# A matrix-vector product on four column tiles: two column blocks side by side, turned by one product of eight columns

## The chip, the cores and the metric

The kernel runs on one core of a Trainium2 chip. The metric is the device time of one execution in microseconds. Engines: TensorE (PE for products, PEld for its weight loads), VectorE (DVE), ScalarE (ACT), GpSimd (POOL) and SyncE (SP), which only issues DMAs here. Each engine runs its own list of instructions in order, and they meet at semaphores.

## What is computed

Two transformer-like blocks run one behind the other over 256 tokens of width 1024, with a context of 256 tokens. Block one: a state-space branch, a pooling branch and a mixture of experts. Block two: two layers of feed-forward, gated linear attention with latent attention, and neighbourhood attention. The change touches only the conditioning: both blocks scale and shift their activations by vectors that come from two condition vectors `c` and `c_ctx`:

```python
mod_l = jnp.split((jax.nn.silu(c) @ w_ada[i] + b_ada[i])[:, None, :], 6, axis=-1)
mod_c = jnp.split((jax.nn.silu(c_ctx) @ w_ada[i] + b_ada[i])[None, None, :], 6, axis=-1)
...
mod_l = jax.nn.silu(c) @ ada_w[l] + ada_b[l]
mod_c = jax.nn.silu(c_ctx) @ ada_w[l] + ada_b[l]
```

`w_ada` is 1024 x 6144, `ada_w` is two matrices of 1024 x 9216, all fp32. The results are needed with the feature on the partition, as `mod1` and `mod2` (128 partitions x tiles x 2).

## The kernel before

The conditioning is cut into 96 chunks of 256 output columns, so two tiles of 128 outputs: 8 in job `first`, 16 in `later`, 36 in each of the two jobs of `ada2`. Job `first` is done before anything else (`T.finish(K.first)`), for the first activations wait for its result. The others are background work: each engine takes one step of the job list at fixed places of its own program (`T.step()`, `S.step()`, `V.step()`): behind each weight tile of a linear product, once per round of the state-space loop (`ssd_pe`, line 1082; 10 rounds in each of 4 groups), once per state and twice per level of the gated linear attention (`gla_pe`, lines 2608 and 2637).

One chunk takes these steps. SP loads its 1024 x 256 weights (1 MB) into one of the three `RAW` buffers of the ring (line 344), as soon as PE has read the tile three places earlier. PE multiplies: for each of the 8 blocks of 128 inputs, `CS[:, k, :]` (128 x 32; columns 0 to 3 are silu of `c`, `c_ctx` and those of block two, the other 28 are zero) is the stationary operand and the weights are the moving one. The output of block k goes to the 32 partitions from `32 * (k % 4)`, that is to one of four column tiles of the array; the products on the four tiles can run side by side. After it each quarter of the bank holds the sum over two blocks, in its rows 0 to 3, for 256 columns. ACT copies the bank to `mrow` (line 520). One step later PE turns it: for each half of the columns `mrow` is the stationary operand and `quarters` the moving one, a 128 x 4 matrix of ones and zeros that adds the four quarters; so 4 columns come out per tile, with the feature on the partition. DVE adds the bias into `mod` (line 530).

So within one step (`conditioning_pe`, line 485) PE does the turn of chunk s-1 and then the row of chunk s. The turn waits for ACT's copy, the row for the weights (`T.ring.landed(j)`) and for a free bank. Banks are handed out in turn, 6 or 8 of them. Every product goes through `T.mm` (line 188 in the profile), every ACT operation through line 313, DVE's `stt` is line 253. An fp32 product stands in the trace as two load records and two product records.

Of the kernel before, what the change touches and what calls it, by code (L numbers as in the profile page):

```python
# [6 lines left out]
F32 = mybir.dt.float32  # L7
# [3 lines left out]
ACT = mybir.ActivationFunctionType  # L11
AX = mybir.AxisListType
MUL, ADD, SUB, MIN, MAX = ALU.mult, ALU.add, ALU.subtract, ALU.min, ALU.max
# [164 lines left out]
class Tensor(Engine):  # L178
# [58 lines left out]
    def conditioning(self, job, s):  # L237
        conditioning_pe(self, self.K, job, s)
# [69 lines left out]
class Scalar(Engine):  # L308
# [3 lines left out]
    def act(self, o, a, f, **k):  # L312
        return self.e.activation(o, a, f, **k) if self.e else NOTHING  # L313
# [21 lines left out]
    def conditioning(self, job, s):  # L335
        conditioning_act(self, self.K, job, s)
# [148 lines left out]
def conditioning_pe(T, K, job, s):  # L485


    pe, act = K.pe, K.act
    if s:
        c = job.base + s - 1  # L490
        b, held = T.bank("turned", c)
        for h in held:
            T.wait_ge(*h)
        T.wait_ge(*act.of("row", c))
        for q in range(2):
            r = T.mm(b[:, 4 * q:4 * q + 4], K.mrow[c % 2][:, q * 128:q * 128 + 128], K.quarters[:, :], True, True)
        r.then_inc(*pe("turned", c))
    if s < job.n:
        c = job.base + s
        j, w = T.weights(job.name, job.lead, 0, 8, job.order[s] * 128, 256, False)  # L500
        T.wait_ge(*T.ring.landed(j))
        b, held = T.bank("row", c)
        for h in held:
            T.wait_ge(*h)
        for k in range(8):
            q = 32 * (k % 4)
            r = T.mm(b[q:q + 32, 0:256], K.CS[:, k, :], w[:, k, :], k < 4, k >= 4)
        r.then_inc(*pe("row", c))
        pe.note("w", T.ring.name, j)


def conditioning_act(S, K, job, s):
    pe, act = K.pe, K.act
    if s < job.n:
        c = job.base + s
        S.take()
        S.wait_ge(*pe.of("row", c))
        if c > 1:
            S.wait_ge(*pe.of("turned", c - 2))
        S.act(K.mrow[c % 2][:, :], K.ps("row", c)[:, 0:256], ACT.Copy).then_inc(*act("row", c))  # L520
        K.free(act, "row", c)


# [146 lines left out]
class Kern:  # L670
    def __init__(self, nc, dram, out, ctx):
# [7 lines left out]
        sb = self.sb  # L679
# [20 lines left out]
        self.mod1 = sb("mod1", [128, 48, 2], F32)  # L700
        self.mod2 = [sb(f"mod2{i}", [128, 72, 2], F32) for i in range(2)]
        self.CS = sb("CS", [128, 8, 32], F32)
        self.quarters = sb("quarters", [128, 4], F32)
        self.mrow = [sb(f"mrow{i}", [128, 256], F32) for i in range(2)]
        self.banks = [ctx.enter_context(nc.psum_tensor(f"ps{i}", [128, 512], F32)) for i in range(8)]
        half = (2, 8)
        self.first = Job("w_ada", None, (0, 8, 2, 10, 4, 12, 6, 14), 0, self.v("b_ada", 0, 48), self.mod1, (), 0)
# [22 lines left out]
    def sb(self, name, shape, dt, ctx=None):  # L730
        return (ctx or self.ctx).enter_context(self.nc.sbuf_tensor(name, shape, dt))
# [45 lines left out]
def setup_dve(V, K):  # L777

    dve, q = K.dve, K.quarters[:, :]
    V.fill(K.CS[:, :, :], 0.0).then_inc(*dve("cs zero"))  # L780
    V.wait_ge(K.loaded["first"], 32)
    V.tt(q, K.ident[:, 0:4], K.ident[:, 32:36], ADD).then_inc(*dve())
    for i in (64, 96):
        V.wait_ge(*dve.last)
        V.tt(q, q, K.ident[:, i:i + 4], ADD).then_inc(*dve("quarters"))
    for key, n in (("b_ada", 1), ("ada_b", 2)):
        for i in range(n):
            for g in ((1, 4), (1, 4, 7))[n - 1]:
                b = K.v(key, 72 * i + 8 * g, 8)
                V.ts(b, b, 1.0, None, ADD).then_inc(*dve())  # L790
            for g in ((), (2, 8))[n - 1]:
                b = K.v(key, 72 * i + 8 * g, 8)
                V.ts(b, b, 0.5, None, MUL).then_inc(*dve())
    V.wait_ge(*dve.last)
# [2721 lines left out]
```

## Time and profile before

| | |
|---|---|
| time, median of 3 runs | 3405.75 us (3403.57 to 3408.22) |
| time of the profiled execution | 3411.45 us |
| its span, first to last instruction | 3409.6 us |
| mean granted TensorE clock | 0.949 of full |
| PE busy | 3090.1 us (91%) |
| PE weight loads busy | 2345.2 us (69%) |
| DVE busy | 1422.5 us (42%) |
| ACT busy | 1091.6 us (32%) |
| POOL busy | 307.5 us (9%) |

Busy shares are over the whole span; the stages differ. By time: 0 to 50 us the chunks of `first`; 50 to 225 the linear products and convolutions of the state-space branch; 225 to 420 the state-space loop; to 1700 the rest of block one and the experts, and the first feed-forward part of block two; 1774 to 1900 the gated linear attention; then the rest. The profiled span lacks 1.85 us of that execution's own time, which lies around it. A duration in a row is that of the record; where several records of one kind overlap, a row of the timeline gives the time from the first start to the last end.

### The profile page before, as it was taken

How to read it: one execution, taken by the hardware profiler on the slowest of the kernel's cores; microseconds unless marked ns; L12 is line 12 of the kernel's file. 1: busy time of each engine (PE TensorE's matmuls, PEld its weight loads, DVE VectorE, ACT ScalarE, POOL GpSimd, SP SyncE). 2: the span in 40 equal slices, each digit the busy share in tenths (PEclk: the TensorE clock that was granted, in tenths of full speed). 3: DMA queues.
4: the chain of work that ended last, by engine and by line, in shares of the span. 5: the costliest groups of instructions: out<-in, count | busy, mean ns of one | idle time of the engine just before them, and what ended most of it. 6: DMA issues, size and time to landing. Idle time of an engine off the chain costs nothing.

```text
span 3409.6 us, 40973 instructions
## 1 busy us (share of the span) xinstructions
PE 3090.1 (91%) x17468; PEld 2345.2 (69%) x17468; DVE 1422.5 (42%) x2099; ACT 1091.6 (32%) x1579; POOL 307.5 (9%) x309
## 2 busy tenths in 40 slices
PE   6988899769999979999898798999989999897998
PEld 4765599745555547787676546878768787773898
DVE  4654554522222234333476454333243333436554
ACT  4443354322222223222342232322242222434433
POOL 0023470100000001000104000000010000300000
PEclk9987899869999989999999899999999999999999
DMA  7456754479999942232239321223222322310453
GB/s 221 156 187 198 225 167 133 121 280 385 395 395 392 387 184 85 77 112 67 82 122 294 97 74 50 96 83 106 74 87 87 99 85 88 136 62 0 131 179 99
DMA packets 415209, 537.16 MB, mean 158 GB/s; under 512 B 14340, under 2 KB 389924, under 8 KB 390308
## 3 DMA queue, kind: packets, MB, share of 16 engines
q1 hardware_dynamic: 415012, 534.38, 46.0%
q8 instruction: 142, 2.33, 0.3%
q14 instruction: 55, 0.45, 0.0%
HBM read 533.30 MB, written 1.05 MB: 157 GB/s over the span
## 4 chain that ended last, share of the span: by engine, by line
PE 82%; DVE 8%; ACT 4%; DMA 3%; issue 2%; SPq 0%; POOL 0%; DVEq 0%; ACTq 0%; POOLq 0%
PE ps L188 80%; PE ps L187 2%; DVE ar L243 2%; ACT ar L313 2%; DMA RAW<-in_ada_w 1%; DVE LR L243 1%; DVE ar L259 1%; ACT HR L313 1%; DMA RAW<-in_w_in 1%; PE ps L194 1%; DVE ar L262 0%; DVE ar L253 0%; DVE ar L249 0%; ACT arf1i L313 0%; ACT AH L313 0%
## 5 line engine op out<-in xcount | busy, mean ns | idle before, releaser
L188 PE MATMUL ps<-AH,HR 128*128 128x512 f32 (+1 forms) x2552 | 901.1, 353 | 64.7 <-DVE AL L243 39.9
L188 PE MATMUL ps<-AL,HR 128*128 128x512 f32 (+1 forms) x2552 | 887.2, 348 | 0.0
L188 PE MATMUL ps<-AH,LR 128*128 128x512 f32 (+1 forms) x2552 | 886.4, 347 | 0.0
L243 DVE TENSOR_TENSOR LR<-RAW,HR 128x2048 fp32r<-128x2048 f32 (+3 forms) x232 | 486.2, 2097 | 601.9 <-ACT HR L313 596.2
L313 ACT ACTIVATE HR<-RAW 128x2048 fp32r<-128x2048 f32 (+3 forms) x232 | 404.1, 1744 | 772.6 <-PE ps L188 666.3
L188 PEld LDWEIGHTS ps<-AH,HR 128*128 128x128 f32 x2552 | 491.3, 193 | 139.8 <-ACT arf1i L313 19.8
L188 PEld LDWEIGHTS ps<-AL,HR 128*128 128x128 f32 x2552 | 491.7, 193 | 59.9 <-issue 1.9
L188 PEld LDWEIGHTS ps<-AH,LR 128*128 128x128 f32 x2552 | 490.9, 192 | 59.0
L188 PE MATMUL ps<-ar 64*128 64x128 f32 (+9 forms) x1318 | 237.7, 370 | 61.7 <-ACT ar L313 26.8
L249 POOL TENSOR_SCALAR X<-X 128x512 f32<-128x512 f32 (+2 forms) x50 | 83.8, 1702 | 2266.0 <-ACT AH L313 1631.8
L188 PEld LDWEIGHTS ps<-ar 64*128 64x128 f32 (+2 forms) x1318 | 140.0, 188 | 147.9 <-issue 47.7
L253 DVE SCALAR_TENSOR_TENSOR X<-ps,mod,X 128x256 f32<-128x256 f32 x152 | 67.4, 480 | 324.5 <-PE ps L188 312.5
L243 POOL TENSOR_TENSOR ar<-ar 128x384 f32<-128x384 f32 (+5 forms) x138 | 151.0, 1103 | 297.8 <-DVE ar L243 117.1
L313 ACT ACTIVATE ar<-ar 128x384 f32<-128x384 f32 (+7 forms) x208 | 109.4, 557 | 164.7 <-DVE ar L249 53.7
L188 PE MATMUL ps<-BHf1i,HR 128*128 128x512 f32 x352 | 147.9, 420 | 11.6 <-DVE BLf1i L243 11.6
L313 ACT ACTIVATE ar<-ps 128x256 f32<-128x256 f32 (+4 forms) x190 | 89.2, 475 | 203.7 <-PE ps L188 195.6
L188 PE MATMUL ps<-BLf1i,HR 128*128 128x512 f32 x352 | 142.5, 405 | 0.0
L188 PE MATMUL ps<-BHf1i,LR 128*128 128x512 f32 x352 | 142.1, 404 | 0.0
L313 ACT ACTIVATE ar_few<-ps 128x512 f32<-128x512 f32 x64 | 47.0, 734 | 286.6 <-PE ps L188 286.6
L188 PE MATMUL ps<-RAW,CS 128*32 128x256 f32 x1536 | 127.4, 459 | 10.4 <-DMA RAW<-in_w_ada 8.2
L188 PE MATMUL ps<-BHf2i,HR 128*128 128x512 f32 (+1 forms) x352 | 124.4, 353 | 9.6 <-DVE BLf2i L243 9.6
L188 PE MATMUL ps<-BLf2i,HR 128*128 128x512 f32 (+1 forms) x352 | 120.4, 342 | 0.0
(181 smaller groups left out, 3778.9 us busy)
## 6 DMA issues: line engine op xcount, KB each, us to landing
RAW<-in_ada_w SPq DMA_DIRECT2D x72, 1024.0 KB, 5.8
RAW<-in_f1i SPq DMA_DIRECT2D x44, 1024.0 KB, 5.1
RAW<-in_f2i SPq DMA_DIRECT2D x44, 1024.0 KB, 5.1
RAW<-in_w_in SPq DMA_DIRECT2D x32, 1024.0 KB, 5.5
RAW<-in_w_ada SPq DMA_DIRECT2D x24, 1024.0 KB, 7.9
RAW<-in_w_eu SPq DMA_DIRECT2D x17, 1024.0 KB, 10.2
HF<-in_w_ed SPq DMA_DIRECT2D x17, 1024.0 KB, 9.2
LF<-in_w_eu SPq DMA_DIRECT2D x17, 1024.0 KB, 10.1
```

The lines of the kernel that those rows point to most:

```text
L187: return self.e.matmul(o, w, x, start=start, stop=stop, skip_group_check=True)
L188: return self.e.matmul(o, w, x, start=start, stop=stop)
L194: return self.e.transpose(o, a, self.K.ident[sp:sp + q, sp:sp + q])
L243: return self.e.tensor_tensor(o, a, b, op) if self.e else NOTHING
L249: return self.e.tensor_scalar(o, a, s1, None, o1)
L253: return self.e.scalar_tensor_tensor(out=o, in0=a, scalar=s, in1=b, op0=o1, op1=o2) if self.e else NOTHING
L259: return self.e.reciprocal(x, x) if self.e else NOTHING
L313: return self.e.activation(o, a, f, **k) if self.e else NOTHING
```

## The change

The row product is laid out anew. The four column tiles now take 128 columns each: tiles 0 and 1 the first 128 output columns of the chunk, tiles 2 and 3 the second 128. Of each pair one tile sums the input blocks 0 to 3 (tile 0, tile 2) and the other the blocks 4 to 7 (tile 1, tile 3). So there are 16 products of 128 columns where there were 8 of 256, and the bank is filled over 128 columns. ACT copies 128 columns, `mrow` is 128 x 128, and one product by `quarters`, now 128 x 8, adds the two half sums of each tile and turns both: columns 0 to 3 are those of the first tile, 4 to 7 those of the second. `quarters` is made by two additions that don't wait for each other, instead of three in a chain. DVE's reading of the turned bank is as it was.

```diff
--- before.py
+++ after.py
@@ -492,9 +492,7 @@
         for h in held:
             T.wait_ge(*h)
         T.wait_ge(*act.of("row", c))
-        for q in range(2):
-            r = T.mm(b[:, 4 * q:4 * q + 4], K.mrow[c % 2][:, q * 128:q * 128 + 128], K.quarters[:, :], True, True)
-        r.then_inc(*pe("turned", c))
+        T.mm(b[:, 0:8], K.mrow[c % 2][:, :], K.quarters[:, :], True, True).then_inc(*pe("turned", c))
     if s < job.n:
         c = job.base + s
         j, w = T.weights(job.name, job.lead, 0, 8, job.order[s] * 128, 256, False)
@@ -502,9 +500,11 @@
         b, held = T.bank("row", c)
         for h in held:
             T.wait_ge(*h)
-        for k in range(8):
-            q = 32 * (k % 4)
-            r = T.mm(b[q:q + 32, 0:256], K.CS[:, k, :], w[:, k, :], k < 4, k >= 4)
+        for k in range(4):
+            for q in range(4):
+                f = k + 4 * (q % 2)
+                r = T.mm(b[32 * q:32 * q + 32, 0:128], K.CS[:, f, :], w[:, f, q // 2 * 128:q // 2 * 128 + 128], k == 0,
+                         k == 3)
         r.then_inc(*pe("row", c))
         pe.note("w", T.ring.name, j)
 
@@ -517,7 +517,7 @@
         S.wait_ge(*pe.of("row", c))
         if c > 1:
             S.wait_ge(*pe.of("turned", c - 2))
-        S.act(K.mrow[c % 2][:, :], K.ps("row", c)[:, 0:256], ACT.Copy).then_inc(*act("row", c))
+        S.act(K.mrow[c % 2][:, :], K.ps("row", c)[:, 0:128], ACT.Copy).then_inc(*act("row", c))
         K.free(act, "row", c)
 
 
@@ -700,8 +700,8 @@
         self.mod1 = sb("mod1", [128, 48, 2], F32)
         self.mod2 = [sb(f"mod2{i}", [128, 72, 2], F32) for i in range(2)]
         self.CS = sb("CS", [128, 8, 32], F32)
-        self.quarters = sb("quarters", [128, 4], F32)
-        self.mrow = [sb(f"mrow{i}", [128, 256], F32) for i in range(2)]
+        self.quarters = sb("quarters", [128, 8], F32)
+        self.mrow = [sb(f"mrow{i}", [128, 128], F32) for i in range(2)]
         self.banks = [ctx.enter_context(nc.psum_tensor(f"ps{i}", [128, 512], F32)) for i in range(8)]
         half = (2, 8)
         self.first = Job("w_ada", None, (0, 8, 2, 10, 4, 12, 6, 14), 0, self.v("b_ada", 0, 48), self.mod1, (), 0)
@@ -779,10 +779,9 @@
     dve, q = K.dve, K.quarters[:, :]
     V.fill(K.CS[:, :, :], 0.0).then_inc(*dve("cs zero"))
     V.wait_ge(K.loaded["first"], 32)
-    V.tt(q, K.ident[:, 0:4], K.ident[:, 32:36], ADD).then_inc(*dve())
-    for i in (64, 96):
-        V.wait_ge(*dve.last)
-        V.tt(q, q, K.ident[:, i:i + 4], ADD).then_inc(*dve("quarters"))
+    for i in range(2):
+        V.tt(q[:, 4 * i:4 * i + 4], K.ident[:, 64 * i:64 * i + 4], K.ident[:, 64 * i + 32:64 * i + 36],
+             ADD).then_inc(*dve("quarters"))
     for key, n in (("b_ada", 1), ("ada_b", 2)):
         for i in range(n):
             for g in ((1, 4), (1, 4, 7))[n - 1]:
```

## Rows read from the trace of the kernel before

**Rows 1.** page, part 4: share of the ending chain by engine.
```profile
PE 82%; DVE 8%; ACT 4%; DMA 3%; issue 2%; SPq 0%; POOL 0%; DVEq 0%; ACTq 0%; POOLq 0%
```

**Rows 2.** groups by shape: names, shape, count | busy us, mean ns | idle.
```profile
L188 PE MATMUL ps<-RAW,CS 128*32 128x256 f32 x1536 | 127.4, 459 | 10.4 <-DMA RAW<-in_w_ada 8.2 <-DMA RAW<-in_ada_w 2.0
...
L188 PE MATMUL ps<-quarters,mrow 128*128 128x4 f32 x384 | 66.4, 279 | 41.6 <-ACT mrow L313 40.4 <-DVE ar L268 1.2
...
L188 PE MATMUL ps<-ar_few 128*128 128x64 f32 x512 | 60.6, 271 | 1.2 <-DVE ar_few L256 1.2
...
L313 ACT ACTIVATE mrow<-ps 128x256 f32<-128x256 f32 x96 | 36.6, 381 | 126.9 <-PE ps L188 109.2 <-DMA X<-in_ctxT 16.0
...
L313 ACT ACTIVATE ar<-ps 128x128 f32<-128x128 f32 x16 | 4.3, 270 | 6.4 <-PE ps L188 6.4
```

**Rows 3.** windows, `mrow` alone: stretch, length, PE, PEld, ACT busy, clock.
```profile
50.00:225.00 175.00, 6.55 (x48) 7.39 (x48) 4.79 (x13) 0.94 0.50 159
225.00:420.00 195.00, 28.82 (x160) 25.33 (x160) 14.99 (x39) 0.82 0.65 210
...
1800.00:1900.00 100.00, 17.88 (x112) 15.81 (x112) 10.74 (x28) 0.89 0.92 288
```

**Rows 4.** timeline, state-space round: start us, duration us, engine, operation, count.
```profile
243.67 0.61 PE L188 MATMUL ps<-quarters,mrow 128*128 128x4 f32 x4
...
244.21 0.59 PEld L188 LDWEIGHTS ps<-RAW,CS 128*32 128x32 f32 x16
244.21 1.07 PE L188 MATMUL ps<-RAW,CS 128*32 128x256 f32 x16
244.23 1.43 POOL L243 TENSOR_TENSOR X<-X,ar 128x256 f32<-128x256 f32 x2 [0.71 <-ACT X L313]
...
245.21 0.65 PE L188 MATMUL ps<-X,ar 128*64 128x256 f32 x4
...
245.61 1.32 POOL L243 TENSOR_TENSOR ar<-ar 128x384 f32<-128x384 f32 x1
...
247.07 0.27 PE L188 MATMUL ps<-quarters,mrow 128*128 128x4 f32 x1
```

**Rows 5.** chain of waits, state-space stage: start us, duration us, what.
```profile
227.22 35.05 PE ps L188 x312
```

**Rows 6.** timeline, linear stage.
```profile
115.60 0.50 PE L188 MATMUL ps<-quarters,mrow 128*128 128x4 f32 x4
...
117.04 0.50 PE L188 MATMUL ps<-AH,HR 128*128 128x512 f32 x1
```

**Rows 7.** chain of waits, first stage.
```profile
23.61 0.39 ACT mrow L313
...
27.00 0.38 ACT mrow L313
...
30.67 0.28 ACT mrow L313
```

**Rows 8.** chain of waits, stage from 1800.
```profile
1815.33 5.15 PE ps L188 x72
...
1821.02 5.15 PE ps L188 x72
...
1845.28 4.64 PE ps L188 x68
...
1849.93 7.33 DMA RAW<-in_ada_w
```

**Rows 9.** timeline, a turn at half clock in the state-space stage.
```profile
230.99 1.02 PE L188 MATMUL ps<-quarters,mrow 128*128 128x4 f32 x4
```

**Rows 10.** records of `ar`: duration min/median/max ns, first and last start.
```profile
L188 PE MATMUL ps<-ar x8: 272/272/324, 1783.5 to 1783.9; 128*64 128x128 f32 x8
```

**Rows 11.** timeline, the same records.
```profile
1783.49 0.66 PE L188 MATMUL ps<-ar 128*64 128x128 f32 x8 [0.23 <-DVE ar L256]
```

**Rows 12.** PE sequencer waits, 242.3 to 242.6: duration ns, first, last start.
```profile
L147 PEldq EVENT_SEMAPHORE  x2: 51/51/51, 242.4 to 242.5; - x2
```

## The prediction, made before the changed kernel was run

> **What bounds the kernel now.** I read the page first. TensorE (PE) makes up 82% of the chain that ended last, so a change to PE work counts wherever PE is what ends last [rows 1]. Then the groups of instructions by shape, for what the change touches: 1536 records of the row products, 384 of the turning products, 96 copies of `mrow` [rows 2]. That is 96 chunks; each fp32 product appears as two records (two passes), so a chunk has 16 row records (8 products) and 4 turning records (2 products). Then the busy time of the turning product and its copy by stage: 8 chunks run before 50 us, 12 turns lie in 50 to 225, 40 in 225 to 420, 28 in 1800 to 1900, and the remaining 8 around these [rows 3]. So three places carry the change, and each has its own limit.
>
> In the state-space stage (225 to 420) one timeline round shows what ends last. The PE records of one round at 2.4 GHz start at 243.67 (turn), 244.21 (row) and 245.21 (next product), and 247.07 is the next turn: 3.40 us with no idle time named before any PE record [rows 4]. POOL works 1.43 + 1.32 = 2.75 us of that, ACT and DVE less. The chain of waits has an unbroken PE piece of 35.05 us over the first group's rounds [rows 5]. Here a nanosecond off PE is a nanosecond off the span. In the linear stage (50 to 225) turn, row and the next linear product follow without idle too, from 115.60 to 117.04 [rows 6].
>
> The first stage is a ring of PE and ACT: the turn waits for the copy of the row, the copy waits for the row [rows 7]. In the stage from 1800 the chain goes through the weight transfers: PE 4.64 us, then 7.33 us of DMA, and so on to the end of the stage [rows 8].
>
> **The turning product: four records become two.** At 2.4 GHz four products take 0.61 us, one alone 0.27, so the pitch is (0.61 - 0.27)/3 = 0.11 us [rows 4]. The pitch is the 128-column load's; that the product has 8 columns instead of 4 adds nothing, since the 64-column products on 128-column weights have about this time too (60.6 us busy over 512 records, 0.118 us each) [rows 2]. Two records off are 0.22 us. At 1.2 GHz four products take 1.02 us [rows 9]; the same 256 clocks of a load are 0.213 there, two off are 0.43 us.
>
> How many of each: the long form (1.0 us for four records instead of 0.50 or 0.61) stands 1 time in the 12 of the linear stage and 11 times in the 40 of the state-space stage. Check with the windows: 29 x 0.61 + 11 x 1.02 = 28.9 us, shown 28.82; 11 x 0.50 + 1.0 = 6.5, shown 6.55 [rows 3]. So linear: 11 x 0.22 + 0.43 = 2.9 us. State space: 29 x 0.22 + 11 x 0.43 = 11.1 us. Both lie on the end.
>
> **The row product: 16 records of 256 columns become 32 of 128.** Four column tiles run side by side. Before, 4 groups of four records; the 16 take 1.07 us, and the next product starts at +1.00 [rows 4]. At two clocks a column a 256-column pass is 0.213 us, and four are 0.853. After, 8 groups of 128 columns, 0.107 us each: the same stream. Nearest rows for such a pass: eight records of 128 x 64 weights by 128 columns on two column tiles, so four groups, take 0.66 us, one 0.27; a pitch of (0.66 - 0.27)/3 = 0.13 with the first group's load in it, some 0.11 without [rows 10, 11]. Eight groups have their last start at 0.13 + 6 x 0.11 = 0.79, and the drain is 0.107 shorter: the next product at about +1.01, against +1.00. At 1.2 GHz both have 1.71 us of stream: equal. Cost 0.01 us a chunk, zero to 1 us in all.
>
> What hides it is that loads and decoding keep up. The 16 loads of a row end within 0.59 us while products of 0.4 us run [rows 4], so they lie beside the stream. Decoding has to bring a load and a product each 27 ns instead of 54. The trace has no stretch of products that dense, so I bound it: between two waits of PE's sequencer at 242.4 and 242.5 the program has the two decay products only, four pairs of records, and their starts are 0.125 us apart by the trace (0.1 us in the row): 31 ns a pair with the 51 ns of the wait charged to them, 18 ns without [rows 12]. I take 18: supply suffices, price 0. The ends kept: 31 ns a pair (row 0.99 instead of 0.86, +0.13) and 54 ns (the densest run shown: these 16, four passes of 0.213 with their gaps, 16 x 0.054 = 0.86 us).
>
> **The copy.** ACT copies 128 columns instead of 256: 0.270 against 0.381 us by the two shapes from PSUM [rows 2], 0.11 less. Where PE is the bound this is covered by PE's work; where ACT is in the ring it counts.
>
> **First stage.** A round of turn, row and copy is 3.39 us, from the copy at 23.61 to that at 27.00. Behind the copy at 27.00 ACT does two scaled inputs until the next copy at 30.67, 3.29 us without a gap, so every other round is ACT's and saves 0.11 only [rows 7]. Seven rounds: four save 0.43 + 0.11, three save 0.11, and the last turn 0.43: 2.9 us. The transfers that it then waits for are issued when a row ends, so they move with it.
>
> **The stage from 1800.** Two pairs of chunks take 4.64 + 7.33 + 0.06 = 12.03 us there, 6.02 a pair, while PE with ACT's copy needed 5.69 a pair before the transfers were late (1815.33 to 1821.02) [rows 8]. Taking 0.22 + 0.22 + 0.11 off that chain enlarges the wait for weights. What is late next is the transfer, which doesn't change. Only the first four pairs, before the transfers are late, give something: I take 1.0 us (bounds 0 and 6.9, all 28 turns).
>
> **The rest.** Six turns from 417 to 1791 would save 1.7; there PE waits for DVE in a step, 0.23 us in one [rows 11], so 1.0. The two behind 2000, one of them at half clock: 0.6. The setup's third DVE addition and its waits lie in the first 8 us, before the first weights land: 0. Banks, waits and DMA issues are the same in number, and none is moved.
>
> **Sum.** 2.9 + 11.1 + 2.9 + 1.0 + 1.0 + 0.6 = 19.5, less 0.5 for the row product: 19 us. Against the profiled execution 3411.45 - 19 = 3392.5; that execution lies 5.7 us over the median of the runs, 3405.75, from which I go: 3386.5 us. A saving ahead of a later stage is carried on, for the later stages start from waits on the earlier ones.
>
> **A rule against the change.** Row: at 244.21 sixteen loads begin and end in 0.59 us while the first products run, so loads on column tiles overlap products [rows 4]. The Trainium skill ("TensorE: Matmul & The Clock Gate", Part 3, "The mechanism") says that a load overlaps products in flight only where the row group differs, and column tiles share theirs. By that rule each of four more groups pays its load; what this would make of the time is the third rival. The trace speaks against it.
>
> **Rivals.**
> 1. *The saving turns into waits.* In the state-space rounds a chain over ACT, DVE and POOL could be the next bound: POOL has 2.75 us of 3.40, 0.43 us of room after the change, but its two operations wait for ACT. If only a third of those 14 us in linear and state space is kept, and the small terms not, the gain is 6 us: 3400. For: POOL's small room. Against: no PE idle time inside the round, which would be there if such a chain were near. Chance 0.13.
> 2. *Decoding at 31 ns a pair.* Rows cost +0.13 at full clock, nothing at half: 40 full-clock blocks x 0.13 = 5, others 2: gain 12, 3393.5. Chance 0.12.
> 3. *Loads exposed.* Four more loads of 0.106 us a row at full clock: +0.42 - 0.22 = +0.20 for 40 turns is +8, about +0.1 for 20 at half clock is +2: 3415. Chance 0.03. It costs time from 0.055 us a load.
> 4. *Decoding is the bound (slower).* If pairs come no faster than the 54 ns of the densest run shown, a full-clock row takes 32 x 0.054 = 1.73 instead of 0.86 us: +0.87 - 0.22 = +0.65, 40 times: +26; at half clock the row already streams 1.73, so -0.43 stays, 20 times: -9; pairs from 1800 take 6.9 instead of 6.03, 13 times: +11; the rest +2. 3436 us. It decides from 34 ns a pair, where 32 r = 0.86 + 0.22. Against: 18 ns above. Chance 0.06. The Trainium skill ("TensorE: Matmul & The Clock Gate", "Wait — 56ns, not 53.3ns?") gives a floor of about 25 ns a product, and 62 where microcode decodes. By the first the forecast stands; by the second a row would take some 1.98 us and the kernel an estimated 3460. The 54 ns of the rows now is under 62, though a queue filled ahead could hide it.
>
> **How the numbers follow.** Forecast 0.66, its own range 3378 to 3394: the stage from 1800 may give up to 4 more or 1 less, and the half clock may last a round longer or shorter in each of the four groups of the state-space stage, some 1 us each (turn +0.4, row and the rest at half speed). About 0.2% (6.8 us) is what a measurement of this kernel can tell from no change. Faster by more: 0.66 + 0.12 + 0.02 of rival 1 = 0.80. Within: 0.11. Slower: 0.03 + 0.06 = 0.09. Range: 3376 to 3401 holds forecast, rivals 1 and 2, less their tails, and leaves rivals 3 and 4 out.
>
> **What would show it.** Turn to row 0.32 us instead of 0.54, row to next 1.00 still, the 3.40 us round at 3.18; 32 row records in 1.07 us; the wait for weights from 1800 longer and the pair still 6.03; copies of 0.27. Row records more than 30 ns apart on average would make rival 2 or 4 true; row to next at 1.4, rival 3; rounds still at 3.40 with PE idle, rival 1.

## The result, and the profile after

The changed kernel takes 3387.75 us (median of 4 runs, 3384.87 to 3389.55), the kernel before beside it 3406.98 us (3403.57 to 3410.83). The ratio is 0.9942, 95% interval 0.9929 to 0.9956: 19.2 us off, between 15 and 24. Run again on another chip it was 3387.73 us, ratio 0.9944 (0.9931 to 0.9957). Forecast: 3386.5 us, 19 off.

| | before | after |
|---|---|---|
| profiled execution's own time, us | 3411.45 | 3386.41 |
| its span, us | 3409.6 | 3384.5 |
| mean granted TensorE clock | 0.949 | 0.951 |
| PE busy, us | 3090.1 | 3059.8 |
| PE records (loads are as many) | 17468 | 18812 |

The spans differ by 25.1 us, more than the medians: the profiled execution of before lies 4.5 us over its median, that of after 1.3 under its own. Differences by place below carry this.

Groups by shape of after (names, shape, count, then busy us and mean ns, then idle time before them); they answer to [rows 2]:

```profile
L188 PE MATMUL ps<-RAW,CS 128*32 128x128 f32 x3072 | 125.3, 314 | 15.7 <-DMA RAW<-in_ada_w 8.0 <-DMA RAW<-in_w_ada 7.7
L188 PE MATMUL ps<-quarters,mrow 128*128 128x8 f32 x192 | 40.4, 283 | 39.6 <-ACT mrow L313 37.2 <-DVE ar L268 2.4
L313 ACT ACTIVATE mrow<-ps 128x128 f32<-128x128 f32 x96 | 26.3, 274 | 115.9 <-PE ps L188 100.0 <-DMA X<-in_ctxT 15.7
```

Twice as many row records need the same busy time (125.3 us, 127.4 before), the turning records fell from 66.4 to 40.4 us, a copy from 381 to 274 ns.

The timeline of after, one round of the state-space stage at full clock (start us, duration us); it answers to [rows 4]:

```profile
243.26 0.39 PE L188 MATMUL ps<-quarters,mrow 128*128 128x8 f32 x2
...
243.58 0.81 PEld L188 LDWEIGHTS ps<-RAW,CS 128*32 128x32 f32 x32
243.58 1.08 PE L188 MATMUL ps<-RAW,CS 128*32 128x128 f32 x32
244.59 0.20 PEld L188 LDWEIGHTS ps<-X,ar 128*64 128x64 f32 x4 [0.20 <-POOL X L243]
...
246.46 0.39 PE L188 MATMUL ps<-quarters,mrow 128*128 128x8 f32 x2
```

Turn to row is 0.32 us (0.54 before), row to next 1.01 (1.00), the round 246.46 - 243.26 = 3.20 us (3.40). The linear stage of after, where the turn to the row is 0.21 us (0.44 in [rows 6]):

```profile
112.75 0.28 PE L188 MATMUL ps<-quarters,mrow 128*128 128x8 f32 x2
112.96 1.08 PE L188 MATMUL ps<-RAW,CS 128*32 128x128 f32 x32
113.97 0.50 PE L188 MATMUL ps<-AH,HR 128*128 128x512 f32 x1
114.31 0.40 PE L188 MATMUL ps<-AL,HR 128*128 128x512 f32 x1
114.55 0.40 PE L188 MATMUL ps<-AH,LR 128*128 128x512 f32 x1
...
115.71 0.40 PE L188 MATMUL ps<-AL,HR 128*128 128x512 f32 x1
```

The chain of waits of after in the first stage, against [rows 7]:

```profile
20.07 2.51 PE ps L188 x34
...
22.60 0.29 ACT mrow L313
...
25.46 0.28 ACT mrow L313
...
29.02 0.17 ACT mrow L313
```

A copy starts 2.86 us behind the one ahead (22.60 to 25.46), and 3.56 in the round where ACT has its scaled inputs to do; before it was 3.39 and 3.67. The stage from 1775, first the waits of PE there (us in total, times, longest), then the timeline around one of them:

```profile
PE ps L188 <- ACT mrow L313: 10.8, 9, 6.9
PE ps L188 <- DMA RAW<-in_ada_w: 8.0, 9, 1.8
```

```profile
1791.38 0.36 PE L188 MATMUL ps<-quarters,mrow 128*128 128x8 f32 x2 [0.49 <-ACT mrow L313]
...
1793.52 1.93 PE L188 MATMUL ps<-RAW,CS 128*32 128x128 f32 x32 [1.78 <-DMA RAW<-in_ada_w]
...
1852.33 1.08 PE L188 MATMUL ps<-RAW,CS 128*32 128x128 f32 x32 [1.52 <-DMA RAW<-in_ada_w]
```

Before, PE waited 2.0 us for these weights, now 8.0: as foretold, the saving enlarges this wait. Not foretold: behind a wait of 1.78 us the row runs 1.93 us instead of 1.08, at half clock. That is not so behind every wait: three of the nine are followed by such a row, the one of 1.52 us isn't, and when the changed kernel was run again it was one (2.29 us) of eleven.

**Where the gain lies.** For the same PE record of the unchanged work, its start in each kernel less its start in the kernel before, from the profiled executions, in us (places by the time of before):

| place | after | after again | one turn, old row | copy of 256 | two turns | filled | before, filled |
|---|---|---|---|---|---|---|---|
| 50 | -3.0 | -2.5 | -2.0 | -2.3 | -1.2 | -2.2 | +0.3 |
| 202 | -3.6 | -3.6 | -3.5 | -4.4 | +0.2 | -3.7 | -0.5 |
| 227 | -2.7 | -4.0 | -2.4 | -4.1 | +0.4 | -4.3 | -4.4 |
| 415 | -22.6 | -25.7 | -19.5 | -20.9 | -1.7 | -39.5 | -32.6 |
| 1774 | -23.2 | -25.5 | -22.8 | -24.2 | -2.9 | -43.8 | -32.3 |
| 1900 | -23.0 | -28.7 | -28.8 | -28.5 | -2.5 | -47.7 | -32.4 |
| end | -25.0 | -28.5 | -29.1 | -24.3 | -2.9 | -47.3 | -34.3 |

Nearly all of it comes between 227 and 415: 17 to 22 us in the four kernels with one turn and no filling. I had 11.1. Each column is one execution, and the first four are each the fastest or second fastest of their kernel, while the one of before that they are set against took longer than any of the four behind its median; so the sums to the end, 24 to 29 us, are larger than what the medians give.

### The profile page after: what moved, and what is told of

Read it like the earlier page. It is cut to its first block, busy times and chain, and to the rows that moved or that the text cites. A ratio compares the mean times of both kernels' runs of the same rounds, so it can differ in the third digit from the quotient of the medians.

```text
span 3384.5 us, 43660 instructions
## 1 busy us (share of the span) xinstructions
PE 3059.8 (90%) x18812; PEld 2365.3 (70%) x18812; DVE 1421.1 (42%) x2098; ACT 1079.3 (32%) x1579; POOL 308.6 (9%) x309
## 4 chain that ended last, share of the span: by engine, by line
PE 82%; DVE 8%; ACT 4%; DMA 3%; issue 2%; SPq 0%; POOL 0%; DVEq 0%; ACTq 0%; POOLq 0%
PE ps L188 79%; PE ps L187 2%; DVE ar L243 2%; ACT ar L313 2%; DVE LR L243 1%; DVE ar L259 1%; DMA RAW<-in_ada_w 1%; ACT HR L313 1%; DMA RAW<-in_w_in 1%; PE ps L194 1%; DVE ar L262 0%; DVE ar L253 0%; DVE ar L249 0%; ACT arf1i L313 0%; ACT AH L313 0%
## 5 line engine op out<-in xcount | busy, mean ns | idle before, releaser
L188 PE MATMUL ps<-RAW,CS 128*32 128x128 f32 x3072 | 125.3, 314 | 15.7 <-DMA RAW<-in_ada_w 8.0
```

The source lines that it names most:

```text
L188: return self.e.matmul(o, w, x, start=start, stop=stop)
```

## The experiments

All ratios are to the kernel before, run on the same chip beside them.

| run | median us (runs) | ratio, 95% interval |
|---|---|---|
| two turns (`e1`) | 3410.03 (11) | 1.0014, 1.0005 to 1.0024 |
| old rows, one turn (`e2`) | 3384.39 (5) | 0.9940, 0.9924 to 0.9956 |
| copy of 256 (`e3`) | 3390.13 (5) | 0.9959, 0.9943 to 0.9975 |
| four turns (`e4`) | 3461.58 (4) | 1.0166, 1.0145 to 1.0188 |
| rows of 64 (`e5`) | 3406.90 (12) | 1.0001, 0.9991 to 1.0012 |
| waits filled (`e6`) | 3370.63 (4) | 0.9900, 0.9881 to 0.9919 |
| one step (`e8`) | 3394.28 (6) | 0.9964, 0.9951 to 0.9977 |
| before, one step (`e9`) | 3421.78 (6) | 1.0046, 1.0028 to 1.0064 |
| before, waits filled (`e10`) | 3383.06 (6) | 0.9940, 0.9921 to 0.9958 |
| after again (`e11`) | 3387.73 (5) | 0.9944, 0.9931 to 0.9957 |
| tile by tile (`e7`) | 3465.95 (2) | 1.0176, 1.0158 to 1.0193 |
| rows of 64, one step (`e12`) | 3400.44 (10) | 0.9981, 0.9970 to 0.9993 |

### Is the turn the whole gain?

Against the changed kernel:

```diff
-        T.mm(b[:, 0:8], K.mrow[c % 2][:, :], K.quarters[:, :], True, True).then_inc(*pe("turned", c))
+        for q in range(2):
+            r = T.mm(b[:, 4 * q:4 * q + 4], K.mrow[c % 2][:, :], K.quarters[:, 4 * q:4 * q + 4], True, True)
+        r.then_inc(*pe("turned", c))
```

> The changed kernel with its new row products and its short copy, but the turn as two products of four columns on the same 128 x 128 `mrow`. Theory: the whole gain comes from the two load-product records fewer in each turn, so this kernel stands at the time of the kernel before, 3405 to 3407 us (ratio 1.000 within 0.001), with turn to row back at 0.54 us and rounds of 3.40 us. Rival: the row's new form or the shorter copy gives a part of the 19 us (by the shorter half clock, which fell in the state-space stage from 71.7 to 51.2 us); then it stands at 3395 to 3401.

It took 3410.03 us: the gain is gone, turn to row is 0.54 us again. The rival (3395 to 3401) is out. But it stands 1.7 to 8 us over the kernel before, where I expected 0.

Against the kernel before, the turn alone:

```diff
-        for q in range(2):
-            r = T.mm(b[:, 4 * q:4 * q + 4], K.mrow[c % 2][:, q * 128:q * 128 + 128], K.quarters[:, :], True, True)
-        r.then_inc(*pe("turned", c))
+        T.mm(b[:, 0:8], K.mrow[c % 2][:, 0:128], K.quarters[:, :], True, True).then_inc(*pe("turned", c))
...
-        self.quarters = sb("quarters", [128, 4], F32)
+        self.quarters = sb("quarters", [128, 8], F32)
```

> The kernel before with its old row products and its copy of 256 columns, and one turning product of eight columns in place of two. It leaves out the values of each chunk's second tile: both tiles get those of the first. Theory: the turn alone brings the gain, 3387 to 3389 us (ratio 0.994 to 0.995 of the kernel before), since the new row takes the same 0.85 us of stream. Rival: the new row has a cost hidden in the result, such as the linear stage's 0.05 us a chunk of slower products behind a row; with the old row that cost is gone, and the time is 3382 to 3384.

3384.39 us, ratio 0.9940, against 0.9942 and 0.9944 for the whole change: the turn alone brings it. Both together say: one product fewer in the turn is worth 20 to 25 us, and the new row with its short copy gives nothing; it may cost up to 5. In the linear stage this cost can be seen. From the row's start to the start of the eighth product behind it, 115.71 - 112.96 = 2.75 us after; before 2.71, with the same product at 118.75 and the row at 116.04:

```profile
116.04 1.07 PE L188 MATMUL ps<-RAW,CS 128*32 128x256 f32 x16
117.04 0.50 PE L188 MATMUL ps<-AH,HR 128*128 128x512 f32 x1
...
118.75 0.39 PE L188 MATMUL ps<-AL,HR 128*128 128x512 f32 x1
```

The copy alone, the changed kernel with ACT writing 256 columns:

```diff
-        S.act(K.mrow[c % 2][:, :], K.ps("row", c)[:, 0:128], ACT.Copy).then_inc(*act("row", c))
+        S.act(K.mrow[c % 2][:, :].rearrange("p (a n) -> p a n", a=2),
+              K.ps("row", c)[:, 0:128].unsqueeze(1).broadcast_to([128, 2, 128]), ACT.Copy).then_inc(*act("row", c))
```

> The changed kernel, with ACT writing 256 columns again (the 128 of the bank twice), of which the turn reads the first 128. Theory: 0.11 us more in the ring of the first stage alone, +0.8 us, and nothing elsewhere: 3388 to 3389. Rival: in the stage from 1800 the copy stands in the chain that ends last as well, 28 times 0.11 = +3 us: 3391.

3390.13 us, 2.4 over the changed kernel, but its interval (0.9943 to 0.9975, so 3386 to 3397 us) holds both forecasts and overlaps that of the changed kernel. The record is 379 ns again. It rules out that the short copy carries the gain, and tells no more.

The changed kernel once more, beside other runs:

> The changed kernel once more, on the chip and beside the runs of the next two. The kernel with the turn undone alone stood 3 to 5 us over the kernel before, so the new row with its short copy may cost something that the sum of the turn hides. Theory: the change is worth 19 us, ratio 0.994, as first measured, and the row costs 0.05 us a chunk in the linear stage and no more than 1 us in all. Rival: the row costs some 4 us, from the stage with the busiest transfers, and the first comparison was a lucky one: ratio 0.9955, 3391.

3387.73 us, ratio 0.9944 (0.9931 to 0.9957): the theory's number to 0.1 us. The rival's 0.9955 lies at the edge of the interval, so a row that costs some 4 us is less likely now, but not out. What the row costs is within what the forecast's sum could bear, and the 1.7 to 8 us of the two-turn kernel over before stay without a place beyond the 0.5 of the linear stage. The sums over all executions, further down, put most of it down to half clock.

### What is one product of a turn worth?

The changed kernel with the turning product issued four times:

```diff
-        T.mm(b[:, 0:8], K.mrow[c % 2][:, :], K.quarters[:, :], True, True).then_inc(*pe("turned", c))
+        for _ in range(4):
+            r = T.mm(b[:, 0:8], K.mrow[c % 2][:, :], K.quarters[:, :], True, True)
+        r.then_inc(*pe("turned", c))
```

> The changed kernel, with the turning product issued four times into the same eight columns, so eight turning records a chunk in place of two. Theory: each further product costs the pitch of its two loads wherever PE ends last, 0.22 us at full clock and 0.43 at half, and once 66 us of half clock shrink or grow with the load; three of them: linear stage +8, state-space stage +36 or more, first stage +8, the stage from 1800 to 6.6 us a pair (+8), the rest +5: 3453 us, up to 3460 with a longer half clock (the two-product turn cost 22 to 25 us over one). Rival: what the removed product cost was mostly the clock (a level that is passed once); then three more cost their bare 0.22 or 0.43 alone and PE waits take up a part: 3430 to 3440.

3461.58 us, 74 over the changed kernel: 24.6 a product, as the two-turn kernel had (22.3). Each costs what the records say:

```profile
256.28 1.06 PE L188 MATMUL ps<-quarters,mrow 128*128 128x8 f32 x8
257.26 1.08 PE L188 MATMUL ps<-RAW,CS 128*32 128x128 f32 x32
```

Eight records hold the row back by 0.98 us, two by 0.32: 0.66 for three products, 0.22 each. The theory's number holds, and the rival is out. The total of 74 is 9 over the sum of its terms, 65, and 1.6 over the longest forecast. By the places of its profile the first stage took 10 us more than in after where I had 8, the linear stage 4 us where I had 8, the state-space stage 31 where I had 36 or more, the stage from 1774 to 1900 took 13 where I had 8, and 11 came between 2000 and 2020, where I had 5 for all the rest; that execution lies 6.7 us under the median.

### Why did the state-space stage give more than 11 us?

The stage's rows by the windows of 225 to 420 (length, PE, PEld, DVE, ACT, POOL busy, granted clock, DMA share, GB/s), for before, two turns, after, after again:

```profile
225.00:420.00 195.00, 172.65 (x1387) 99.92 (x1388) 98.69 (x264) 70.77 (x178) 86.70 (x97) 0.82 0.65 210
```

```profile
225.00:420.00 195.00, 174.86 (x2012) 121.83 (x2010) 98.97 (x265) 67.08 (x179) 86.55 (x96) 0.81 0.66 213
```

```profile
225.00:420.00 195.00, 176.43 (x2109) 127.77 (x2108) 103.21 (x264) 74.48 (x189) 88.84 (x100) 0.87 0.75 241
```

```profile
225.00:420.00 195.00, 176.24 (x2135) 129.97 (x2126) 103.26 (x264) 76.35 (x190) 90.24 (x104) 0.89 0.76 245
```

A mean of 0.82 with the two levels 1 and 0.5 is 0.36 of the window at half clock, 70 us; 0.87 is 0.26, 51 us. The other kernels with one turn show 0.86 and 0.87, the others with two 0.81. So half clock shrinks by some 20 us, and where PE ends last each such microsecond costs half of one: 10 us more. With 40 turns at 0.22 that is 8.8 + 10 = 19. This window reaches past the end of the stage in the faster kernels. Between the same two products, 227 and 415 us in before, the trace's clock records give 70 us at half clock of 188 before, 69 of 186 with two turns, and 47, 43, 53 and 54 of 166 to 171 in the four kernels with one. Take half of it off each length, and 152.9 and 151.7 us are left with two turns, 144.2 to 144.7 with one: some 8.5 us less work at full clock, which is the turn, and 8 to 13 us of clock.

What sets it off shows ahead of a group's first round. The timeline of PE in after, and below it in the kernel of the next experiment (whose line numbers are one higher):

```profile
265.19 1.04 PE L194 MATMUL ps<-ident,ar 128*128 128x128 f32 x8
268.68 0.70 PE L188 MATMUL ps<-ar,ident 32*128 32x256 f32 x4 [2.45 <-DVE ar L243]
269.31 0.39 PE L188 MATMUL ps<-quarters,mrow 128*128 128x8 f32 x2
269.63 1.15 PE L188 MATMUL ps<-RAW,CS 128*32 128x128 f32 x32
270.70 1.22 PE L188 MATMUL ps<-ar,ident 32*128 32x256 f32 x4
271.86 0.59 PE L188 MATMUL ps<-quarters,mrow 128*128 128x8 f32 x2
```

```profile
260.31 1.46 PE L189 MATMUL ps<-ar,onesD 128*128 128x256 f32 x6
262.93 0.70 PE L189 MATMUL ps<-ar,ident 32*128 32x256 f32 x4 [1.16 <-DVE ar L244]
263.56 0.39 PE L189 MATMUL ps<-quarters,mrow 128*128 128x8 f32 x2
263.88 1.08 PE L189 MATMUL ps<-RAW,CS 128*32 128x128 f32 x32
264.89 0.70 PE L189 MATMUL ps<-ar,ident 32*128 32x256 f32 x4
265.52 0.39 PE L189 MATMUL ps<-quarters,mrow 128*128 128x8 f32 x2
```

In after PE stands still for 2.45 us, and a round later the same four records take 1.22 us instead of 0.70.

The kernel before has the same waits, though: seven of 2.14 or 2.46 us between the two places, 16 us in all, in both. What differs is what comes behind them. Before, half clock follows each of the seven; in after it follows the four long ones and only the last of the three of 2.14 us. Behind one of these in before (granted clock 0.50 from 266.4 to 269.8):

```profile
265.64 6.26 PE L188 MATMUL ps<-ar 128*128 128x512 f32 x12 [2.14 <-DVE ar L243]
```

Why one turn instead of two spares these, no run shows. It isn't simply the length of a round: with four turns half clock is 64 us between the two places, with the order of products exchanged, further down, 17. So the 20 us less come again in every kernel with one turn, but nobody could have counted them from the trace of before.

The edit, ahead of each of the two waits in each group (`fill(g, 0)`, `fill(g, 1)`), with `FILL = 3`:

```diff
+    def fill(g, i):
+        b, held = T.bank("fill", g, i)
+        for w in held:
+            T.wait_ge(*w)
+        for _ in range(FILL):
+            r = T.mm(b[:, 0:256], K.onesD[:, :], o.CT[:, g, :], True, True)
+        r.then_inc(*pe("fill", g, i))
+        K.free(pe, "fill", g, i)
...
+        fill(g, 0)
         T.wait_ge(*dve.of("xdc", g))
...
+        fill(g, 1)
         T.wait_ge(*dve.of("xdl", g))
```

> The changed kernel, with three idle products of 256 columns ahead of each of the two waits for DVE at the start of each of the four groups of the state-space loop (their results are not read). Theory: the half clock in this stage (51 us between 225 and 420, a window of some 10 us behind each group's start) is set off by PE standing still at these waits, and the shorter half clock is where the state-space stage gave 19.8 us instead of the 11.1 predicted; with the waits filled, most of it goes: 30 to 50 us less half clock, each worth half its length where PE ends last, 3365 to 3378. Rival: the half clock does not hang on these waits, or the filling takes what it gives: 3386 to 3392.

3370.63 us, ratio 0.9900: 17 us faster than the changed kernel and 36 than before, the fastest kernel of this study, with more work in it. The clock of the stage went to 0.98:

```profile
225.00:420.00 195.00, 180.10 (x2239) 137.24 (x2240) 111.20 (x268) 82.61 (x200) 101.00 (x119) 0.98 0.80 255
```

The same in the kernel before separates the two parts of the change's worth:

> The kernel before, with the same idle products ahead of the two waits of each group as the changed kernel had in the run with filled waits (3370.6 us, half clock between 200 and 425 us down from 61 to 14). Theory: with the clock held up the state-space stage has almost only full-clock turns, and the change is worth 40 x 0.22 = 8.8 us there and not 16 to 20; so this kernel stands 13 to 17 us over the filled changed one: 3384 to 3388, and its own gain over the kernel before is 18 to 22 us. Rival: the change's worth doesn't hang on the half clock: 19 us or more over the filled changed one, 3389 to 3395.

3383.06 us, 12.4 over the filled changed kernel by the medians, 13.0 by the spans (3375.3 against 3362.3), just under the 13 to 17 of the theory. Its clock is nearly as high:

```profile
225.00:420.00 195.00, 185.02 (x1669) 126.15 (x1666) 110.13 (x265) 86.89 (x195) 94.95 (x110) 0.96 0.78 251
```

Between 227 and 415 the two filled kernels differ by 35.2 - 28.2 = 7.0 us, where 40 turns at 0.22 would be 8.8; without filling it was 17 to 22. So the large part of the difference that went was clock. The 7.0 is not the bare turn either. A round at full clock is 3.40 us in the one and 3.19 in the other, 8.4 us in forty; half clock is still 12 us between the two places in the one and 3 in the other, up to 4.5 us of time; and in the filled changed kernel PE waits longer, 5.3 us for ACT near the stage's end against 2.9, and 5 times for weights, 1.7 us, where neither the filled kernel before nor the changed one without filling does (with rounds of 3.19 us and a transfer of 1 MB in each, which takes 3.01). How these add up to 7.0 one profile each doesn't tell. By the medians alone the rival (19 us or more) isn't out either: the two intervals leave 5 to 22 us for the difference.

```profile
PE ps L189 <- DMA RAW<-in_ada_w: 1.7, 5, 0.5
```

The executions that have no trace can be used as well, for each has its span and mean granted clock on record. As far as PE is what ends last, span times clock is the time that the execution would have taken at full clock all through, and the rest is what half clock took. Means in us, good to about 1 in the first column and 1 to 4 in the second:

| kernel (executions) | at full clock | taken by half clock |
|---|---|---|
| before (59) | 3234.4 | 169.9 |
| changed (9) | 3222.5 | 162.5 |
| two turns (11) | 3234.9 | 173.2 |
| one turn, old row (5) | 3217.6 | 165.8 |
| four turns (4) | 3271.8 | 187.7 |
| rows of 64 (12) | 3231.8 | 171.9 |
| changed, filled (4) | 3227.9 | 140.6 |
| before, filled (6) | 3235.7 | 146.6 |
| changed, one step (6) | 3221.5 | 171.9 |
| before, one step (6) | 3237.8 | 182.4 |

So of the change's 19 us some 12 are work and some 7 are clock. Between the filled kernels it is 7.8 and 6.0: filling makes the clock's part smaller, it doesn't take it away. A product in the turn costs (3271.8 - 3222.5)/3 = 16.4 us of work, and 8.4 of clock. The new row costs 4.9 us of work by the two kernels with one turn and 0.5 by the two with two turns, which leaves open what it costs.

### The stage from 1775

One step per half level in place of two (`T.step(2)`, `S.step(2)`, `V.step(2)` become single steps), in the changed kernel and in the one before:

> The changed kernel, with one step of the conditioning jobs per half level of the gated linear attention in place of two, so that half of these chunks with their 1 MB transfers move into the loops behind it. Theory: from 1800 a pair of chunks can't go faster than its two transfers (6.02 us), and the saving of the turn is lost there; with half the transfers the levels go by VectorE's chain, 5.9 us each, the waits for weights of 8 us go, and the windows of half clock behind them: 5 to 10 us less in that stage, 3378 to 3383, if the moved chunks cost no more behind it. Rival: the moved chunks lie on the end in their new place (14 times 1.3 us, less what they stop costing): 3390 to 3400.

> The kernel before with the same one step per half level. Against the changed kernel with one step it tells what the change is worth when the stage from 1800 is not bound by its transfers. Theory: the turns moved behind give their 0.22 to 0.43 us there, so the change is worth 22 to 26 us here instead of 19: with the changed one at 3380, this one at 3403 to 3406. Rival: the change's worth is the same in both places, 19 us.

3394.28 and 3421.78 us. My theory missed in both: the changed kernel with single steps is 6.5 us slower than with two, not 5 to 10 faster. By the profile it gains 20 us on the kernel before from 1774 to 1900 and then loses 24 from 2000 to 2100, where the moved chunks lie on the end, as the rival has it. Of the 20 us, 8 come before 1817 and 10 behind 1882; the levels between gained little. The chain of waits goes over DVE and ACT there, as the theory had it (5.9 us), at 5.80 us a level against 6.02 with two steps, and PE waits for POOL:

```profile
PE ps L188 <- POOL ar L243: 25.2, 12, 5.6
```

The change is worth 27.5 us with single steps (0.9964 against 1.0046; the intervals leave 20 to 35) and 19 with two: more than my 22 to 26 by the medians, in the direction of the theory. 14 chunks at 0.22 to 0.43 explain 3 to 6 of these 8 us. By the table of all executions it is 16.3 us of work (11.9 with two steps) and 10.5 of clock (7.4), so both parts grew.

In the two-step kernels the stage from 1774 to 1900 gave +0.2, -3.2, -6.0 and -4.3 us in four profiles of one-turn kernels (columns one to four of the table), and +0.4 with two turns. The transfers bound it in all of them. One difference between the first two is how many rows run at half clock behind a wait for weights, three and one. With one profile each, I leave it at: between nothing and 6 us.

### How near is the row to the limit of supply?

The changed kernel with each row product cut in two:

```diff
-        for k in range(4):
-            for q in range(4):
-                f = k + 4 * (q % 2)
-                r = T.mm(b[32 * q:32 * q + 32, 0:128], K.CS[:, f, :], w[:, f, q // 2 * 128:q // 2 * 128 + 128], k == 0,
-                         k == 3)
+        for u in range(2):
+            for k in range(4):
+                for q in range(4):
+                    f, at = k + 4 * (q % 2), q // 2 * 128 + 64 * u
+                    r = T.mm(b[32 * q:32 * q + 32, 64 * u:64 * u + 64], K.CS[:, f, :], w[:, f, at:at + 64], k == 0,
+                             k == 3)
```

> The changed kernel, with each row product cut into two of 64 columns: 64 load-product record pairs a row in place of 32, the same 0.85 us of stream at full clock, 13 ns a pair. It tells how near the new row is to the limit of supply. If pairs come every 18 ns (the value I took), a row takes 64 x 0.018 = 1.15 us, +0.3 for some 45 rows at full clock that lie on the end: +14 us, 3401. If every 25 to 27 ns (the new row then runs just at its limit), 1.6 to 1.73 us, +0.75 to +0.87: +34 to +40 us, some at half clock too, 3420 to 3430. If pairs come faster than 13 ns and loads stay hidden, no change: 3388.

In the state-space stage a row with twice the records takes the same time:

```profile
242.42 0.94 PEld L188 LDWEIGHTS ps<-RAW,CS 128*32 128x32 f32 x64
242.42 1.10 PE L188 MATMUL ps<-RAW,CS 128*32 128x64 f32 x64
243.45 0.20 PEld L188 LDWEIGHTS ps<-X,ar 128*64 128x64 f32 x4
```

64 pairs of load and product in 1.03 us, 16 ns a pair. The starts in the trace are 6 or 7 ns apart within a group of four and 56 ns from group to group, so even this row goes at the pace of its 64 columns, and the limit of supply lies further down. Rivals 2 and 4 needed pairs of 31 and 54 ns. And yet the kernel takes 3406.90 us (3394.1 to 3412.9), 19 over the changed one, and the third forecast (no change) is as wrong as the first two: not the row is longer, something else. By the table of all executions 9.3 us of the 19 are work and 9.4 are clock. The profiled execution is the fastest of the twelve, 12.8 us under the median; by its places the stage from 1774 to 1900 takes 8 to 11 us more than in the two profiles of the changed kernel, and the state-space stage 4 to 6. The waits of PE from 1775 to 1900, and one place:

```profile
PE ps L188 <- issue: 12.0, 11, 1.7
```

```profile
1830.01 0.53 PE L188 MATMUL ps<-RAW,CS 128*32 128x64 f32 x20 [0.98 <-issue]
```

"issue" is idle time for which the profile knows no releaser. In the kernels before and after there is none in this stretch. What grew with the records is the queue that fetches instructions, after and then rows of 64 (packets, MB, share):

```profile
q8 instruction: 153, 2.51, 0.3%
```

```profile
q8 instruction: 177, 2.90, 0.4%
```

If PE's instructions come late because the transfers of weights fill the same engines, the standstills should go where these are thinner. Hence the rows of 64 with one step per half level:

> The rows of 64 columns (64 record pairs a row) together with one step of the jobs per half level, so that the same rows meet transfers half as dense. With the rows of 64 PE stood still without any wait that the profile shows for 12.0 us, 11 times, in the stage from 1775 to 1900, where the transfers run without pause (28 rows), and for 2.4 us in the 195 us of the state-space stage (40 rows at 0.73 DMA share). Theory: PE's instructions come by the same DMA engines as the weights and are late where these are full; with 14 rows at half the density the standstills in the levels all but go (under 1.5 us), and the kernel stands at the time of the one with one step alone, 3394 to 3398. Rival: they hang on the number of instructions in a row, whatever the transfers do: 14 rows of 28 keep half of them, 5 to 6 us there and as much behind, and the time is 3405 to 3412.

The waits of PE from 1775 to 1900 hold no "issue" at all (28 rows became 14, the DMA share is 0.42; it was 0.77 with two steps):

```profile
PE ps L188 <- POOL ar L243: 28.4, 13, 5.6
```

Half as many rows should have kept 5 to 6 us of it by the rival. At 1900 the profile stands within 0.7 us of that of the one-step kernel, and their spans are equal. The median, 3400.44 us, is 6 over the other's, outside my 3394 to 3398 and outside the rival's 3405 to 3412; since the profiled execution of the one-step kernel lies 6 us over its own median, no profile shows where these 6 are. In the state-space stage, at a DMA share of 0.72, 3.0 us of "issue" remain (2.4 at 0.73 with two steps). So: the standstills go with dense transfers and not with the number of rows alone, in one profile of each kernel; that it is the fetch of instructions that is late is the likeliest reading, and no record shows it by itself.

### Does the order of the products matter?

The changed kernel with the two loops of the row exchanged, `for q in range(4)` outside:

> The changed kernel with the loops of the row exchanged: the four products of one column tile behind each other, and then those of the next tile, in place of one on each tile in turn. Same products, same sizes, same bank. Theory: products overlap only with neighbours on another tile, in the order in which they stand; each tile's eight passes of 0.107 us then run alone, and a row takes about 3.4 us at full clock instead of 1.0: +2.4 us for the 60 rows on the end, the rows from 1800 at 9 to 10 us a pair and those of the first stage too: +190 to +230 us, 3580 to 3620. Rival: TensorE keeps a queue for each tile and lets later products pass, so the order does not matter: 3388.

3465.95 us, +78, and between the two forecasts (+200, 0):

```profile
242.67 2.46 PE L188 MATMUL ps<-RAW,CS 128*32 128x128 f32 x32
245.06 0.48 PE L188 MATMUL ps<-ar,ident 32*128 32x256 f32 x2
```

A row holds PE 2.39 us instead of 1.01, and not 3.4. The starts within a row at 145.58 us form four trains of eight with a pitch of 109 ns; the second begins 466 ns behind the first, the third at 933, the fourth at 1400, each just after the train ahead has started its fifth. So products for another tile do pass those waiting for their own, but only over a few. By the pattern alone, since the records don't name their tile. One on each tile in turn is worth 1.38 us a row. The two executions come to 3322.0 us at full clock and 142.0 taken by half clock, so the order costs 99.5 us of work, and 20.5 come back by the clock.

## Why the prediction was right, and where it was off

The kind and the total were right: 19 us forecast, 19.2 and 18.5 measured. Term by term less so.

- **The turn, -0.22 us.** Right, to 0.01: 0.54 to 0.32 in the rounds, 0.44 to 0.21 in the linear stage, and 0.22 a product with four. At half clock 0.95 to 0.53 us. In the state-space stage, of the 39 turns with a row behind them, 28 ran at full clock and 11 at half before, 29 and 10 after, so the count that I had taken from before held; turn to row summed over them fell from 25.6 to 14.6 us, 11.0 where I had 11.1.
- **The row, +0.01, "the same stream".** The record is right (1.01 against 1.00, eight groups at a pitch of 109 ns). What I left out is what PE does after it: the products behind a row run up to 0.01 us further apart for some ten of them, 0.04 to 0.05 us a chunk. Row and copy together may cost up to 5 us, where I allowed 1.
- **First stage, -2.9.** The rounds are as worked out: 3.39 to 2.86 (-0.53, forecast -0.54) and 3.67 to 3.56 (-0.11). At 50 us the four kernels are ahead by 2.0 to 3.0.
- **Linear stage, -2.9.** Too large: 12 x 0.17 = 2.0 by the records with that 0.05 off; over the stage the profiles show 0.6 to 2.1.
- **State space, -11.1.** The term that was mis-sized: 17 to 22 us in the profiles. The turns gave their 11 as worked out. What I had at nothing in the sum, and at up to 4 us in the range ("a round longer or shorter" in each group, "some 1 us each"), is all other work of PE in this stage, of which less ran at half clock: that gave the rest, 6 to 11 us. Half clock fell by 16 to 27 us of 70 in all, and with most of it gone in both kernels the same stage gave 7.0. Why it fell stays open.
- **From 1775, -1.0.** The mechanism was right: weights are late (2.0 to 8.0 us of waits), the transfers bound the pair. Off: such a wait can be followed by a row at half clock (three of nine in one profile, one of eleven in the other), so a saved microsecond that turns into a wait can cost on top. The first profile gives +0.2, the others up to -6.0.
- **Rival 1** (savings turn into waits) is out: no new waits within the rounds. **Rival 2 and 4** (supply of 31 or 54 ns a pair): the pairs come every 16 ns. **Rival 3** (loads exposed): loads of 0.81 us lie within the row's 1.08.
- **The sum.** By place the profiles add up to 24 to 29 us, the medians to 19. 5.8 of this is that the profiled execution of before lies over its median and that of after under it. I had set the sum against the median, rightly; in which stage these us sit, one profile doesn't say. Over all executions the 19 us are some 12 of work and 7 of clock. So the kind of the effect and the turn's price were foreseen, and that the total came out to 0.2 us is partly luck: the clock's share outside the turns, which I had not counted, stood against terms that were too large (the linear stage, the row).

The Trainium skill ("TensorE: Matmul & The Clock Gate", section "Wait — 56ns, not 53.3ns?") gives about 25 ns from start to start as the least for however small a product, and the prediction leant on it against rival 4. By that floor 64 products of 64 columns would take an estimated 1.6 us; the row took 1.03. On four column tiles the measurement decides: 16 ns on average, 6 or 7 within a group of four.

## What to carry to other kernels

A load-bound product in a stage where PE ends last costs its 0.11 us a record, and can be counted from the timeline. But ask beside it what each microsecond does to the granted clock, for in this kernel that was 7 of the 19 us: look ahead of every stretch at half clock for the wait that comes before it, and try a few idle products there (17 us for 24 products). Before leaning on one profile, multiply span and granted clock of every execution: over 59 of the kernel before, the product has a standard deviation of 2.1 us, the time one of 4.0. And before splitting products into more and smaller ones, look at the DMA share of that stage: where transfers filled it, twice the records cost 19 us, half of it clock, although each row took no longer.

## What was not expected of the hardware

- Half clock can follow a standstill of PE: 2.45 us of wait for DVE, and 2.0 us after PE resumed the same four records take 1.22 us instead of 0.70; 1.78 us of wait for weights, and the row behind it takes 1.93. It need not: two of three waits of 2.14 us and one of 1.52 had nothing behind them in the same profile. With six records of 256 columns in the gap the remaining wait of 1.16 us had no such effect here.
- Load and product pairs on four column tiles start 16 ns apart on average (64 in 1.03 us), 6 or 7 ns within a group of four.
- With transfers at 0.77 of the DMA engines PE stood still 11 times for up to 1.7 us with nothing to wait for that the profile shows, once it had 64 pairs a row; at 0.42 in the same stage never.
- By the pattern of their starts, products for one column tile overtake others that wait for theirs, over about four.
